# One decoder layer on one core: first conditioning in feature groups with carried projections, and another order of weights, stores and gathers around the experts

## What is computed

```
mod = silu(c) @ w_ada + b_ada             # 9 conditioning rows (1 prompt, 8 samples) of 6*1024
sh1, sc1, g1, sh2, sc2, g2 = split(mod)
h = x * (1 + sc1) + sh1
z = h @ w_in + b_in                       # a, a_gate (512 each), q, k, v, indexer q/k/weights, u, v, gates
y_a = silu(LN(depthwise_conv31(a * sigmoid(a_gate))))
y_b = top-k sparse attention(...);  y_c = chunked spatial gating(u, v)
x = LN(alpha*x + (1+g1) * ((sum of gated projections of y_a, y_b, y_c) @ w_o))
h2 = x*(1+sc2)+sh2
x = LN(alpha*x + (1+g2) * moe(h2))        # 16 experts of width 512, each token goes to 2
```

## Time and profile before

| | us |
|---|---|
| median of 3 runs (1125.71 to 1134.81) | 1132.91 |
| the profiled execution, whole | 1129.62 |
| its span in the profile | 1127.8 |

### The profile page before, as it was taken

The page is one execution under the profiler, slowest core; times in us unless marked ns, Lnnn a source line. Parts: engine busy times, 40 slices in busy tenths (PEclk is TensorE's granted clock), DMA queues, the critical chain, the costliest instruction groups (busy, mean ns, idle before and its releaser), DMA issues. The chain is left out here.

```text
span 1127.8 us, 22134 instructions
## 1 busy us (share of the span) xinstructions
PE 1004.3 (89%) x8978; PEld 673.7 (60%) x8978; DVE 490.9 (44%) x1259; ACT 186.9 (17%) x451; POOL 231.3 (21%) x260
## 2 busy tenths in 40 slices
PE   4699999998899998999999999976999999998930
PEld 3477777544776666677777764564655555554510
DVE  0211799982447788865114004676133011110118
ACT  2200012112222211221111110111111111111102
POOL 1300012635221122313325440001000000000044
PEclk9799999999998998999999999986999999999965
DMA  9932643647604305114072317133879999999864
GB/s 310 339 62 77 198 151 112 227 152 283 225 24 140 76 28 166 49 43 118 10 184 60 112 45 301 66 117 160 320 288 358 383 419 367 387 391 398 323 154 122
DMA packets 93572, 218.43 MB, mean 194 GB/s; under 512 B 23696, under 2 KB 42503, under 8 KB 89373
## 3 DMA queue, kind: packets, MB, share of 16 engines
q1 hardware_dynamic: 71428, 183.83, 45.3%
q0 software_dynamic: 5936, 19.16, 5.2%
q10 hardware_dynamic: 16113, 14.06, 4.2%
HBM read 198.95 MB, written 21.06 MB: 195 GB/s over the span
## 5 line engine op out<-in xcount | busy, mean ns | idle before, releaser
L1642 PE MATMUL bank<-arena 128*128 128x288 f32 (+5 forms) x2034 | 510.3, 408 | 8.7 <-issue 4.2
L1642 PEld LDWEIGHTS bank<-arena 128*128 128x128 f32 (+1 forms) x2034 | 371.3, 193 | 138.7 <-issue 49.4
L2005 PE MATMUL bank<-arena 128*32 128x256 f32 x3136 | 181.8, 383 | 11.4 <-issue 7.6
L2005 PEld LDWEIGHTS bank<-arena 128*32 128x32 f32 x3136 | 103.8, 109 | 81.2 <-issue 15.0
L1593 DVE TENSOR_TENSOR arena<-arena,bank 128x128 f32<-128x128 f32 x49 | 14.2, 290 | 235.9 <-ACT arena L1063 235.8
L2024 PE MATMUL bank<-arena 128*32 128x256 f32 x1568 | 94.6, 381 | 0.0
L801 POOL TENSOR_SCALAR arena<-arena 128x288 f32<-128x288 f32 x48 | 46.2, 963 | 218.6 <-ACT arena L1025 218.6
L1137 DVE SCALAR_TENSOR_TENSOR arena<-arena 128x512 f32<-128x512 f32 x120 | 82.0, 746 | 0.0
L1646 PE MATMUL bank<-arena 128*128 128x128 f32 (+6 forms) x327 | 51.2, 294 | 33.3 <-DMA arena<-in_x_sample 9.2
L1646 PEld LDWEIGHTS bank<-arena 128*128 128x128 f32 (+6 forms) x327 | 39.2, 156 | 47.8 <-issue 18.7
L2024 PEld LDWEIGHTS bank<-arena 128*32 128x32 f32 x1568 | 45.9, 108 | 31.9 <-issue 2.0
(11 more groups left out here) (266 smaller groups left out, 835.3 us busy)
## 6 DMA issues: line engine op xcount, KB each, us to landing
arena<-in_w_e_gate SPq DMA_DIRECT2D x16, 2048.0 KB, 11.4
arena<-in_w_e_up SPq DMA_DIRECT2D x16, 2048.0 KB, 16.1
arena<-in_w_e_down SPq DMA_DIRECT2D x16, 2048.0 KB, 10.8
arena<-in_w_ada SPq DMA_DIRECT2D x12, 2048.0 KB, 12.3
arena<-in_w_in SPq DMA_DIRECT2D x10, 2048.0 KB, 10.5
expert_rows<-arena POOLq DMA_DIRECT2D x1, 5120.0 KB, 18.5
arena<-in_x_prompt SPq DMA_DIRECT2D x8, 512.0 KB, 5.4
expert_rows<-arena ACTq DMA_DIRECT2D x28, 96.0 KB, 7.4
```

What stands on the lines that cost most here:

```text
L1642: last = pe.matmul(out, a, b, start=k == 0, stop=k == len(pairs_) - 1)
L2005: last = pe.matmul(out, HG[:, g % 2, k, a:a + BLK], gate_up[i % 2][:, :, k, c * P:c * P + P], start=k == 0, stop=k == KT - 1)
```

## The change

**Start.** The first 2048 columns of `w_ada` come in four groups `("adp", g)`: 256 columns of sh1 and the matching 256 of sc1, by two DMAs of 1 MB, each into a buffer of its own. The `a` columns of `w_in` come as four row blocks of 256 features x 1024 columns (1 MB). The queue is: c, constants, group 0, x, rows 0, group 1, rows 1, group 2, rows 2, group 3, rows 3, with no wait between. The bias of these columns comes as 16 rows and is transposed with the other parameters, and DVE adds it when it takes a group's transposed result; POOL has no part in it. Each group makes two feature tiles of `HT` ready (one by DVE, one by ACT, each 512 wide), and PE at once adds these tiles to six products (`EARLY`, steps `acc`, function `carry`) that stay open in six banks. The last tile closes them. x's tiles are now copied by ACT and DVE in turn.

**Experts and around.** Down weights get a third slot (`A_DOWN3`), so down of turn i waits for `down` of turn i-3, from turn 3 on. `BC2` is loaded before turn 9. Gate and up of turn 1 are issued ahead of the store of the last 64 rows of h2. DVE finishes h2 in two halves, and PE transposes each when it is there. ACT stores every block by itself, with one DMA. At the end POOL alternates: three first gathers, then second and first in turn.

The core of the diff:

```diff
-    plan = [("cT",)] + [("xT", f) for f in range(KT)] + [("xTs",), ("ada", 0), ("ck",), ("par",), ("ada", 1), ("mT", 0)]
-    plan += [("ada", 2), ("mT", 1), ("ada", 3), ("mT", 2), ("mT", 3)]
+    plan = [("cT",), ("adp", 0), ("par",), ("mT", 0)] + [("xT", f) for f in range(KT)] + [("xTs",), ("mod", 0)]
+    for g in range(3):
+        plan += [("acc", 2 * g, 0, 6), ("adp", g + 1), ("acc", 2 * g + 1, 0, 3), ("mT", g + 1), ("mod", g + 1), ("acc", 2 * g + 1, 3, 6)]
+    plan += [("acc", 6, 0, 6)]
...
+EARLY = [("fm", "ag", 0, 0), ("fm", "ag", 0, 1), ("fm", "a", 0, 0), ("fm", "a", 0, 1), ("fm", "ag", 1, 0), ("fm", "ag", 1, 1)]
...
-    w = [(("ada", 0), 0), (("ada", 1), 1), (("ada", 2), 2), (("ada", 3), 0), (("a", 1), 1), (("a", 0), 2), (("q",), 0), (("ada", 4), 1), (("k",), 2)]
+    w = [(("adp", 0), 0), (("a",), 1), (("q",), 0), (("ada", 4), 1), (("k",), 2)]
...
+    down_ring = [ring[2], ring[5], V(A_DOWN3, SLOT)]
+
+    def expert_down(sp, e, z):
+
+        w = I["w_e_down"][0]
+        w = w[e] if type(e) is int else w[bass.ds(e, 1)].rearrange("e k n -> (e k) n")
+        sp.dma_start(down_ring[z].rearrange("p (k n) -> p k n", k=NJ), w.rearrange("(k p) n -> p k n", p=P)).then_inc(ev(f"down_in{z}"), 16)
...
+        def first_conditioning(g):
+            for z in range(2):
+                a = D * z + 256 * g
+                sp.dma_start(adp_buf[g][:, :, 256 * z:256 * z + 256], I["w_ada"][0][:, a:a + 256].rearrange("(k p) n -> p k n", p=P)).then_inc(ev(f"adp_in{g}"), 16)
+
+        first_conditioning(0)
...
+        for g in range(4):
+            if g:
+                first_conditioning(g)
+            sp.dma_start(a_rows[:, 2 * g:2 * g + 2, :], I["w_in"][0][256 * g:256 * g + 256, 0:1024].rearrange("(k p) n -> p k n", p=P)).then_inc(ev(f"a_in{g}"), 16)
...
-                for z in range(3):
-                    expert_weights(sp, 0, z)
+                expert_weights(sp, 0, 0)
+                expert_weights(sp, 0, 1)
+                expert_down(sp, 0, 0)
             if t >= 1:
-                sp.wait_ge(ev("h2_ready"), t)
+                sp.wait_ge(ev("h2_ready"), 2 * t)
                 sp.dma_start(h2_d[(t - 1) * P:t * P, :], H2[:, (t - 1) % 2, :]).then_inc(ev(f"h2_out{(t - 1) % 2}"), 16)
-        sp.wait_ge(ev("h2_ready"), NT)
+        sp.wait_ge(slot_out, rel[("wo", 1)])
+        expert_weights(sp, 1, 3)
+        expert_weights(sp, 1, 4)
+        sp.wait_ge(ev("h2_ready"), 2 * NT)
         sp.dma_start(h2_d[SEQ:NTOK, :], H2[0:NS, 0, :]).then_inc(ev("h2_out0"), 16)
-
-        sp.wait_ge(slot_out, rel[("wo", 1)])
-        for z in range(3):
...
-            if i == 5:
+            if i == 9:
...
-            sp.wait_ge(ev("dn_full"), FIRST[i - 1])
-            expert_weights(sp, e, z + 2)
+            if i >= 3:
+                sp.wait_ge(ev("dn_full"), FIRST[i - 2])
+            else:
+
+                sp.wait_ge(ev("weights_up"), 1)
+            expert_down(sp, e, i % 3)
...
+        for t in range(NT + 2):
+            if t < NT:
+                first_rows(t)
+            if t >= 2:
+                second_rows(t - 2)
...
+            elif kind == "adp":
+                g = key[1]
+                act.wait_ge(*tt.full(key))
+                if g >= 2:
+                    act.wait_ge(*tt.full(("mT", g - 2)))
+                act.activation(MB[:, g % 2, :], tt.tile(key)[:, 0:P], ACT.Copy).then_inc(tt.free(key), 1)
...
+            elif kind == "mod":
+                g = key[1]
+                f = 2 * g + 1
+                act.wait_ge(ev("modT_up"), g + 1)
+                act.wait_ge(*tt.taken(("xT", f)))
...
-                if d in ends:
-                    act.wait_ge(ev("yo_up"), d + 1)
-                    rows = y_d[FIRST[i] * BLK:FIRST[i + 1] * BLK, :].rearrange("(b t) f -> t b f", t=BLK)
-                    for c in range(4):
-                        act.dma_start(rows[:, :, 256 * c:256 * c + 256], YR[BLK * c:BLK * c + BLK, i % 2, 0:NB_AT[i], :]).then_inc(ev(f"yo_out{i % 2}"), 16)
+                y = YR[:, i % 2, d - FIRST[i], :]
+                act.activation(y, banks[6 + d % 2][:, 0:256], ACT.Copy, scale=WBLK[:, d:d + 1]).then_inc(ev("yo_up"), 1)
+                act.wait_ge(ev("yo_up"), d + 1)
+
+                act.dma_start(bass.AP(y_d.tensor, d * BLK * D, [[256, 4], [D, BLK], [1, 256]]), y).then_inc(ev(f"yo_out{i % 2}"), 16)
         nov = act.value_load(ints[0:1, I_NOV:I_NOV + 1], min_val=0, max_val=NOV)
...
+        def modulate(g):
+
+            f, two = 2 * g, slice(2 * g, 2 * g + 2)
+            dve.wait_ge(*tt.taken(("xT", f)))
+            done(ts(HT[:, f, 0:SEQ], HT[:, f, 0:SEQ], MT[:, 8 + f, 0:1], MT[:, f, 0:1], ALU.mult, ALU.add))
+            new = HT[:, two, SEQ:NTOK].rearrange("p f (b t) -> p f b t", t=ST)
+            per_sample = lambda z: MT[:, z + 2 * g:z + 2 * g + 2, 1:9].unsqueeze(3).broadcast_to([P, 2, NB, ST])
+            link(tt_(new, new, per_sample(KT), ALU.mult))
+            link(tt_(new, new, per_sample(0), ALU.add))
...
-                    stt(h2, h2, rs, BC["sh" + pick][0:n], ALU.mult, ALU.add).then_inc(ev("h2_ready"), 1)
+                    for z in range(2):
+                        c2 = slice(512 * z, 512 * z + 512)
+                        stt(h2[:, c2], h2[:, c2], rs, BC["sh" + pick][0:n, c2], ALU.mult, ALU.add).then_inc(ev("h2_ready"), 1)
...
+        def carry(key, k):
+            _, name, j, h = key
+            a = (512 if name == "ag" else 0) + j * P
+            return pe.matmul(early_in(key).tile(key)[:, 0:HALF], a_rows[:, k, a:a + P], HT[:, k, h * HALF:h * HALF + HALF], start=k == 0, stop=k == KT - 1)
...
+            if kind == "acc":
+                _, f, i0, i1 = key
+                pe.wait_ge(ev("ht_dve"), f // 2 + 1)
+                if f % 2:
+                    pe.wait_ge(ev("ht_act"), f // 2 + 1)
+                pe.wait_ge(ev(f"a_in{f // 2}"), 16)
+                for k2 in EARLY[i0:i1]:
+                    carry(k2, f)
+                continue
...
+            elif kind == "adp":
+                g = key[1]
+                if g == 0:
+                    pe.wait_ge(*tt.taken(("cT",)))
+                pe.wait_ge(ev(f"adp_in{g}"), 32)
+                for k in range(KT):
+                    for q in range(4):
+                        last = pe.matmul(ps[32 * q:32 * q + 32, 0:P], CTP[:, k, :], adp_buf[g][:, k, q * P:q * P + P], start=k == 0, stop=k == KT - 1)
...
```

212 lines of the change are left out of this document (115 added, 97 removed).

## The result

| | us |
|---|---|
| before, median of 10 runs (1123.62 to 1136.54) | 1132.58 |
| changed kernel, median of 10 runs (1136.69 to 1150.15) | 1138.26 |
| ratio, 95% interval | 1.0086 (1.0059 to 1.0112) |
| forecast | 1110, range 1099 to 1122 |
| the changed kernel's profiled execution, its span | 1150.15, 1148.3 |

The medians alone are 5.7 us apart; the ratio is worth 9.7 us. One execution of the kernel with turn stores and the late down took 2094.53 us, where its nine others took 1116.60 to 1125.72; its ratio leaves it out.

What follows compares the result with a forecast made beforehand. It took the start as bound by bytes, the experts as losing 11.8 us to PE's stops, and the end as a DVE chain. Gains 11 + 7.5 + 2 + 2 = 22.5 us gave 1110, range 1099 to 1122.

Steps and rivals of the forecast that it cites:

- The store: Experts: ACT's store after every block fits its 2.98 us idle time, since earlier issues took 0.45, 1.73 at most.
- Slower: Experts: store issue outlasts ACT's idle time, delaying each of 49 blocks; 1159 us at an issue of 4; chance 0.04.
- The start: Kernel start: reordered loads and carried products end the products 11 us earlier; from below nothing, from above 20.4.
- the 19.5 of the walk: Start: arrival time of x in us, reckoned 19.2 from bytes ahead and taken as 19.5 for shared engines.
- the three pauses of 0.6: Start: PE waits about 0.6 us three times, 1.8 in all, while group columns pass ACT, PE and DVE.
- the 1.4 for a late group 3: Start: group 3 of `w_ada` comes about 1.4 us late for PE.
- the 1.1 a group of the walk: Start: 1 KB segments of `w_ada` cost 0 to 1.4 us a group; 1.1 taken.
- The middle: From 60 to 300 us: work starts from the products, so an earlier start shifts it all and reaches the end.
- The gather before the experts: Ahead of the experts: gate and up of turn 1 issued some 7 us earlier; gain 2 us, from -3 to +3.3.
- The experts without the store: Experts: PE's stops ahead of turns 4, 6, 8 and 13 shrink, gaining 7.5 us; bounds 3 and 11.8.
- turn 13: Experts: earlier down load of turn 12 cuts the 4.55 us stop to 0.8 to 1.1; slow block (1.7) goes.
- The end: Kernel end: one last store instead of four and alternating gathers start things earlier; gain 2 us, bounds 1.3 and 4.

Runs made afterwards that it cites:

- the kernel with turn stores and the late down: Changed kernel with the four DMAs per turn of before, and down issued only when the turn before's first down block is done: 1122.42 us, ratio 0.9915.
- turn stores: Changed kernel with the stores of before, four DMAs of 32 partitions after a turn's last block, instead of one DMA per block: 1117.84 us, ratio 0.9889.

## Why the prediction was wrong

**The store** is the step that failed. The prediction took "ACT stores after each block" as a matter of issue time: from the earlier trace rows 0.45 in the middle and 1.73 at most, against 2.98 of idle time. Those rows are of DMAs over 32 partitions with another access pattern. For the new DMA no row stood there, and I took the nearest without asking what differed: the outermost dimension of the address, 32 before, 4 now. The rival "Slower" named the engine and the way (ACT's issue takes longer than its idle time, PE late behind it), but priced it as an equal delay in each of 49 blocks and gave it 0.04; it came as 0.58 us in most and 3.8 to 13.6 us in nine, and as waits for landings that no rival named. "DMA: Bandwidth & Descriptors" in the Trainium skill, which I had cited for its segments, has the rule (section "Why a DMA increments its semaphore by 16 and not by 1"); by it the store has a quarter of the engines, and this rival the larger chance. The price: 1.0086 against 0.9889, 22.3 us on 1130.

**The start, 11 predicted, 7.5 measured.** That is by the mark of ada 4; in the whole time the start alone gave 4.4 (1.4 to 7.4). The mechanism is right, as the profile shows it: carried products with little between them, groups hidden behind them. Mis-sized were the terms ahead of them. x arrived 1.8 us later than the 19.5 of the walk (21.27; 21.8 to 22.7 in the others), with the 2.1 MB of group 0 ahead of it. From the first transpose to the first carried product I had 7.8; it took 9.7, of which 2.06 is a pause for the modulation. And the first six products ran at 1.2 GHz, 6.03 us instead of 2.9. In the profiles of this start the group took 3.19 to 6.07: how much of a cold start is paid is chance. The other way, the three pauses of 0.6 and the 1.4 for a late group 3 did not come: from 31 us to the last carried product PE has no pause over 0.2 us. So groups 1 to 3 were not waited for; what segments of 1 KB cost, the 1.1 a group of the walk, no run shows. The change itself had a wrong order: x behind group 0 costs 4 us (ada 4 at 107.9 against 112.0).

**The middle** passed the lead on, as far as the means tell: 555.8 against 555.6.

**The gather before the experts, 2 predicted, 3.2 measured** (98.2 to 98.4 from the router's weights to the first `hidden` in most profiles with this part, 101.4 before). PE waited 5.12 us for the first gather (8.43 before), whose landing took 4.34 where the earlier trace rows has 7.66; the last h2 rows behind 4 MB did not hold it up.

**The experts without the store, 7.5 predicted, 2 to 4 measured** (five profiles that have this part of the change as it is and stores that don't stall take 302.3 to 304.7, mean 303.8, and a sixth, with four stores a block, 306.1; before 305.6, with the new start alone 307.6). With turn stores the stop at turn 8 is 0.7 and that at turn 6 under 1, as forecast or better. The step that failed is turn 13: "Now that load stands right behind gate and up of turn 12, some 12 us earlier, and is nearly done when gate 13 is issued". It is not done early enough to matter, since from turn 9 on the queue never empties: a three-block turn takes 17.7 us for 6.3 MB of weights, 0.4 of rows (half a MB in four blocks) and 0.4 of stores, 400 GB/s of the 419 that the window above shows. A load moved ahead within that full queue brought turn 13 nothing (4.02 and 3.95). The trace of before had it, in windows of 50 us that I did not weigh (DMA share and GB/s last):

```profile
950.00:1000.00 50.00, 50.00 (x857) 28.63 (x853) 5.79 (x20) 7.55 (x20) 1.87 (x2) 1.00 0.96 383
1000.00:1050.00 50.00, 45.45 (x751) 26.39 (x747) 6.09 (x18) 6.87 (x17) 0.94 (x1) 0.97 1.00 399
```

**The end, 2 predicted, 1.5 measured** in the changed kernel; with turn stores from 0.7 less than before to 0.4 more. The new store put into the kernel before, with its old gathers, gave 1.2 (46.1), so nearly all of the 1.5 is the store's, and the new order of gathers gave little. DVE starts 2.4 to 3.4 us earlier, as predicted, and gives most of it back, because a tile's second gather waits for its own first, and POOL with it.

**Sum as it should have been:** with turn stores 7.5 + 3.2 + 2 + 0.4 = 13.1 (measured 12.5 by the ratio), less 22.3 for the new store, its gain at the end included: 9 us slower. The ratio says 9.7, the medians 5.7.

## What to carry to other kernels

Ahead of a new DMA write down its access pattern outermost first on both sides, and how many engines that gives; a store whose issue takes 0.58 us can still stop the engine that issues it for 13.6, when the stores ahead of it don't drain. Moving a load earlier from one full stretch into another brought nothing here, so look at the DMA share of both stretches before giving it a buffer. And a gain at the head of a pipeline (DVE starting earlier at the end) counts only if the next tiles keep pace: check the second tile, too.
